# Weights split a unit ahead, low parts written over their landing slots, and a second mixer that begins with half of its value columns

## What is computed

```python
for i in range(DEPTH):                      # DEPTH = 2
    mix = ssd_mixer(x, ...) if i == 0 else hgrn2_mixer(x, ...)
    h = layer_norm(ALPHA * x + mix, ln_g[i, 0], ln_b[i, 0])
    h = layer_norm(ALPHA * h + square(relu(h @ mlp_w1[i])) @ mlp_w2[i], ln_g[i, 1], ln_b[i, 1])
    x = h + sigmoid(h @ ple_w_gate[i]) * (p[i] @ ple_w_proj[i])
```

## Time and profile before

| | |
|---|---|
| median of 3 runs | 2112.82 us (2112.81 to 2113.82) |
| the profiled execution's own time | 2113.44 us |
| its span in the profile | 2111.6 us |
| mean granted clock of PE | 0.967 |
| PE busy | 1975.9 us (94%) |
| DVE busy | 1072.6 us (51%) |
| ACT busy | 871.8 us (41%) |
| POOL busy | 173.3 us (8%) |

### The profile page before, as it was taken

One profiled execution on the slowest core, in us unless ns is written; L12 is line 12 of the kernel. 1 busy time (PEld: TensorE's weight loads), 2 busy tenths in 40 slices (PEclk: granted clock), 3 DMA queues, 4 the chain that ended last, 5 costly groups with the idle time before them and its releaser, 6 DMA issues.

```text
span 2111.6 us, 26519 instructions
## 1 busy us (share of the span) xinstructions
PE 1975.9 (94%) x9594; PEld 1572.8 (74%) x9594; DVE 1072.6 (51%) x1891; ACT 871.8 (41%) x1734; POOL 173.3 (8%) x137
## 2 busy tenths in 40 slices
PE   7999999979999999899898689999999879989998
PEld 6788887878888887688888577888887655447773
DVE  4666666355344344467677554343446342035643
ACT  5665664253333225366575534233334220114430
POOL 0110110030000003001010040000004000001100
PEclk9999999999999999999999799999999979988999
DMA  5131124313232220413121122222231212110010
GB/s 186 41 100 60 41 80 156 123 61 120 80 118 81 96 103 20 120 42 79 40 80 41 60 88 93 80 103 96 81 118 45 86 53 100 64 40 1 0 40 40
DMA packets 116542, 161.31 MB, mean 76 GB/s; under 512 B 6021, under 2 KB 57059, under 8 KB 116451
## 3 DMA queue, kind: packets, MB, share of 16 engines
q1 hardware_dynamic: 115155, 155.38, 22.1%
q0 software_dynamic: 1296, 4.72, 0.6%
HBM read 157.98 MB, written 2.10 MB: 76 GB/s over the span
## 4 chain that ended last, share of the span: by engine, by line
PE 82%; DVE 9%; ACT 5%; issue 2%; DVEq 1%; ACTq 1%; DMA 0%; SPq 0%; POOLq 0%; POOL 0%
PE psum L885 42%; PE psum L660 8%; PE psum L986 7%; PE psum L1141 4%; PE psum L625 4%; PE psum L848 3%; PE psum L1222 2%; PE psum L1176 2%; PE psum L1018 2%; PE psum L1189 2%; PE psum L965 1%; PE psum L809 1%; DVE z_lo L1782 1%; DVE w_lo L1992 1%; ACT fT L1279 1%
## 5 line engine op out<-in xcount | busy, mean ns | idle before, releaser
L1992 DVE TENSOR_TENSOR w_lo<-slot,w_hi 128x512 fp32r<-128x512 f32 x304 | 214.0, 719 | 377.4 <-ACT w_hi L1448 377.4
L1448 ACT CAST w_hi<-slot 128x512 fp32r<-128x512 f32 x304 | 183.7, 620 | 446.9 <-PE psum L885 446.2
L885 PE MATMUL psum<-f_hi,w_hi 128*128 128x512 f32 (+1 forms) x576 | 214.4, 372 | 21.4 <-issue 8.5
L885 PE MATMUL psum<-f_lo,w_hi 128*128 128x512 f32 (+1 forms) x576 | 213.5, 371 | 0.0
L885 PE MATMUL psum<-f_hi,w_lo 128*128 128x512 f32 (+1 forms) x576 | 213.2, 370 | 0.0
L885 PE MATMUL psum<-w_hi,hid_hi 128*128 128x512 f32 x512 | 199.5, 390 | 0.0
L885 PE MATMUL psum<-w_hi,hid_lo 128*128 128x512 f32 x512 | 199.2, 389 | 0.0
L885 PE MATMUL psum<-w_lo,hid_hi 128*128 128x512 f32 x512 | 199.2, 389 | 0.0
L885 PEld LDWEIGHTS psum<-f_hi,w_hi 128*128 128x128 f32 x576 | 111.7, 194 | 40.2 <-issue 8.9
L625 PE MATMUL psum<-con,arena 128*128 128x128 f32 (+2 forms) x710 | 106.1, 288 | 23.4 <-ACT arena L1695 8.2
L885 PEld LDWEIGHTS psum<-f_hi,w_lo 128*128 128x128 f32 x576 | 111.7, 194 | 17.6
(11 more groups left out here) (309 smaller groups left out, 4118.9 us busy)
## 6 DMA issues: line engine op xcount, KB each, us to landing
slot<-in_w_mlp SPq DMA_DIRECT2D x128, 512.0 KB, 5.5
slot<-in_w_ssd SPq DMA_DIRECT2D x32, 512.0 KB, 5.6
slot<-in_w_hgrn SPq DMA_DIRECT2D x32, 512.0 KB, 6.6
slot<-in_w_ssd_out SPq DMA_DIRECT2D x16, 512.0 KB, 6.2
slot<-in_w_gate SPq DMA_DIRECT2D x16, 512.0 KB, 5.2
gb<-in_w_ssd SPq DMA_DIRECT2D x8, 512.0 KB, 8.3
slot<-in_w_hgrn_out SPq DMA_DIRECT2D x8, 512.0 KB, 5.3
slot<-in_w_mla SPq DMA_DIRECT2D x8, 512.0 KB, 5.5
```

The costliest lines, as they stand in the source:

```text
L885: m = pe.matmul(psum[:, bank[c], cols or slice(0, HALF)], a, m_, start=opens and k == 0 and n_pass == 0, stop=closes and k == KD - 1 and n ...
L1448: act.copy(w_hi[:, k, :], as_k(slot_of(stage, n))[:, k, :]).then_inc(high_made, 1)
L1992: dve.tensor_tensor(w_lo[:, k, :], as_k(slot_of(stage, n))[:, k, :], w_hi[:, k, :].bitcast(F32), ALU.subtract).then_inc(low_made, 1)
```

## The change

High parts get two buffers (`w_his`; the second lies where `w_lo` was). The low parts lose theirs: `w_los` are views of the two landing slots, and DVE writes the low part over the landed values. A split now waits for PE's blocks of two units before; a slot is given back piece by piece, as PE begins the block behind a piece.

DVE no longer splits the next unit in one go ahead of tile 3, but in portions behind each of the four norms: 2, 2, 1, 3 blocks before an MLP, 3, 3, 2, 0 before a gate. ACT makes all eight high parts behind the square root of tile 0, and takes half of the turned values ahead of each root. In an MLP's first half product the turn of tile 3 moves to the middle (`halfway`). In `ssd_out` the last two tiles of the second half trade banks.

The second mixer's first weights are split in the order 2, 0, 1, on ACT ahead of the turned values, on DVE inside `ple` behind tile 1. PE projects part 2 once two tiles are ready, turns tile 3 behind it, and then makes parts 0, 1, 3 (before: 0, 1, 2, 3).

```diff
+MLP_SPLITS, GATE_SPLITS = (2, 2, 1, 3), (3, 3, 2, 0)
...
-        w_hi, w_lo = part("w_hi", 17920, KD, HALF), part("w_lo", 22016, KD, HALF)
+        w_his = [part(f"w_hi{n}", 17920 + n * KD * HALF, KD, HALF) for n in range(2)]
+        w_los = [x_lo, z_lo]
...
+                    if by_piece:
+
+                        sp.wait_ge(blocks_begun, split_units.index(u - 2) * KD + ((c + 1) * step + 1) + i * (per * KD))
+                        sp.sem_inc(sig("slot_given"), 1)
                     sp.dma_start(dst[:, c * step:(c + 1) * step, :], w(c * step, step)).then_inc(done, 16)
...
-                up(0, 0, slice(0, T // 2), ends=False)
-                last_turn()
+                up(0, 0, slice(0, T // 2), ends=False, halfway=last_turn)
...
-            for n in range(4):
-                hgrn_project(0, 0, n)
+            for t in range(NT - 1):
+                turn_rows("turn0", res, t, sig("ple_done0"), t + 1)
+            input_ready(2)
+            hgrn_project(0, 0, 2, 0)
+            turn_rows("turn0", res, NT - 1, sig("ple_done0"), NT)
+            input_ready(NT)
+            hgrn_project(0, 0, 0, 1)
+            hgrn_project(0, 0, 1, 2)
+            hgrn_project(0, 0, 3)
...
-                        act.wait_ge(blocks_begun, (u - 1) * KD + (k + 2) + i * (per * KD))
-                    act.copy(w_hi[:, k, :], as_k(slot_of(stage, n))[:, k, :]).then_inc(high_made, 1)
+                        act.wait_ge(blocks_begun, (u - 2) * KD + (k + 2) + i * (per * KD))
+                    act.copy(parts_of(stage, n)[0][:, k, :], as_k(slot_of(stage, n))[:, k, :]).then_inc(high_made, 1)
...
+                    if t > 0 and parts:
+                        turned_out(stage, t - 1, gain, bias)
...
+                    if t == 0 and split_next:
+                        split_next()
...
+            landed(act, "hgrn", 0)
+            for c in (2, 0, 1):
+                split_cols_high(0, c)
             for t in range(NT):
                 turned_out("turn0", t)
                 input_parts("turn0", t)
-                if t == 1:
-                    landed(act, "hgrn", 0)
-                    split_cols_high(0, 0)
-            split_cols_high(0, 1)
-            split_cols_high(0, 2)
...
-                        if before_last:
-                            before_last()
                     add(t)
                     dve.drain()
                     norm(t, rn[:, t, :], rn[:, t, :], LN_EPS, True).then_inc(norm_ready, 1)
                     if 1 < t < NT - 1:
                         input_parts(t - 2)
-                    if t == 1 and meanwhile:
-                        meanwhile()
+                    split_low(split_next, ks=range(sum(counts[:t]), sum(counts[:t + 1])))
...
+                    if t == 1 and meanwhile:
+                        meanwhile()
...
+            ple(0, first_cols_low)
```

More of the change, by code:

```diff
@@ L482, in load @@
             def load(view, w, stage, n=0, i=0, per=0):
-                s, done = slot_free(stage, n, i, per)
+                u = unit0[stage] + n
+                by_piece = stage in in_parts and u - 2 in split_units
+                s, done = (slots[u % 2], units_landed[u % 2]) if by_piece else slot_free(stage, n, i, per)
                 nk = view[1]
@@ L879, in times_parts @@
                         ready(k)
+                    if halfway and k == KD // 2:
+                        halfway()
                     for c in cs:
@@ L947, in gate_results @@
                 def gate_results(h, **results):
+                    w_hi, w_lo = parts_of(f"gate{i}", h)
                     times_parts(f"gate{i}", h, lambda t, k: (f_hi[:, k, t * P:(t + 1) * P], f_lo[:, k, t * P:(t + 1) * P],
@@ L971, in _, with hgrn_project @@
             ple(0, mlp(0, last_turn))
[L972 to L977, removed]
+            input_ready = next_input()
+            def hgrn_project(par, i, n, nth=None):
                 h = 2 * i + par
+                w_hi, w_lo = w_his
                 if n < 3:
-                    pe.wait_ge(sig("cols_low"), h * 3 + (n + 1))
+                    pe.wait_ge(sig("cols_low"), h * 3 + ((n if nth is None else nth) + 1))
                 def passes(out, hi_lo, k):
@@ L1455, in input_parts, with norm @@
                 act.copy(f_hi[:, :, tokens], fT[:, :, tokens]).then_inc(input_high, 1)
-            def norm(stage=None, gain=None, bias=None, parts=False, meanwhile=None, before_last=None):
+            def norm(stage=None, gain=None, bias=None, parts=False, split_next=None):
                 n = norms[0]
@@ L1512, in mlp @@
                 quarter(QUARTERS - 1, last=True)
-                norm(f"norm{i}1", B_G + 16 * i + 8, B_B + 16 * i + 8, parts=True, before_last=lambda: split_high(f"gate{i}"))
+                norm(f"norm{i}1", B_G + 16 * i + 8, B_B + 16 * i + 8, parts=True, split_next=lambda: split_high(f"gate{i}"))
             def ple(i):
@@ L1520, in ple @@
                         act.activation(sg[:, t, h * HALF:(h + 1) * HALF], psum[:, b, :], ACT.Sigmoid).then_inc(bank_free[b], 1)
-            norm("norm00", B_G, B_B, parts=True, before_last=lambda: split_high("mlp0"))
+            norm("norm00", B_G, B_B, parts=True, split_next=lambda: split_high("mlp0"))
             for i in range(DEPTH):
@@ L1646, in _ @@
                 act.copy(o_hi[:, k, :], oT[:, k, :]).then_inc(sig("o_high"), 1)
-            split_high("hgrn_out", 1)
-            norm("norm10", B_G + 16, B_B + 16, parts=True, before_last=lambda: split_high("mlp1"))
+            split_high("hgrn_out", 1, follows=False)
+            norm("norm10", B_G + 16, B_B + 16, parts=True, split_next=lambda: split_high("mlp1"))
             mlp(1)
@@ L1985, in _, with split_low @@
             inputs_split = [0]
-            def split_low(stage, n=0, i=0, per=0):
+            def split_low(stage, n=0, i=0, per=0, ks=range(KD)):
                 first = (part0[stage] + n) * KD
-                for k in range(KD):
+                w_hi, w_lo = parts_of(stage, n)
+                for k in ks:
                     dve.wait_ge(high_made, first + (k + 1) + i * (per * KD))
@@ L2101, in last_out_low, with split_cols_low, first_cols_low @@
                     out_low(3, k)
[L2103 to L2104 removed]
+            mixer_and_norm("ssd_out", "mlp0", last_out_low)
             mlp(0)
[L2106 to L2109 removed]
+            def split_cols_low(par, h, c, nth=None):
+                dve.wait_ge(sig("cols_high"), h * 3 + ((c if nth is None else nth) + 1))
                 cols = slice(c * P, (c + 1 + (c == 2)) * P)
+                w_hi, w_lo = w_his
                 dve.tensor_tensor(w_lo[:, :, cols], as_k(slot_of("hgrn", par))[:, :, cols], w_hi[:, :, cols].bitcast(F32),
                                   ALU.subtract).then_inc(sig("cols_low"), 1)
+            def first_cols_low():
+                for nth, c in enumerate((2, 0, 1)):
+                    split_cols_low(0, 0, c, nth)
+            ple(0, first_cols_low)
             for t in range(NT):
@@ L2254, in _ @@
             split_low("hgrn_out", 1)
-            mixer_and_norm("hgrn_out", name=lambda h, t: ((h, t), 0),
-                           before_last=lambda: split_low("mlp1"))
+            mixer_and_norm("hgrn_out", "mlp1")
             mlp(1)
```

55 lines of the change are left out of this document (22 added, 33 removed).

## The result

The changed kernel takes 2141.93 us (median; 2140.74 to 2142.62) where the kernel before takes 2112.82: a ratio of 1.0137, 95% interval 1.0119 to 1.0154. It is slower, as forecast, but by 29 us and not by 9, and it lies 5 us above the upper end of the range. Its profiled execution has a span of 2140.8 us, 29.2 more than that of before.

What follows compares the result with a forecast made beforehand. PE, busy 94%, was taken to bound the kernel, with changes only at four norm stretches and the second mixer's start. 4.4 + 8.4 - 5.5 - 5.5 - 10.5 = -8.7 us: 2112.8 becomes 2121.5 us, range 2104 to 2137.

Steps and rivals of the forecast that it cites:

- the low part over the slot is the same instruction with another address: Low parts written over the landing slots: listed among what was costed at nothing.
- only three things can change the time: PE, busy 94% of 2111.6 us: only a wait removed, a wait added, or a stretch at another clock matters.
- Turns of DVE and POOL: Norm stretches: two-SBUF-operand DVE instructions and POOL's run one after the other; about twenty low parts of 2.5 to 2.9 us.
- Before the MLPs: Norm stretches ahead of `mlp0` and `mlp1`: PE starts earlier, gains of 4.4 and 8.4 us.
- Before the gates: Ahead of `gate0` and `gate1`: late additions make PE wait, loss 4.3 us each, up to 2.8 more; taken 5.5 twice.
- Second mixer: Its start: PE pauses behind v and g and before the first level; loss 9.7 to 12.5 us, taken 10.5.
- Rival 1: Norm stretches: low parts slip past POOL and additions are on time; 33 us faster, 2080 us; chance 0.12.
- Rival 4: MLPs: slots come back late and each of 32 units waits 1 us; 2150 us; chance 0.03.
- Rival 3: Gates go worse: cold clocks in every new pause, PE behind DVE for all the first head; 2131 to 2138 us; chance 0.10.

Runs made afterwards that it cites:

- m2_offsets: Matmuls alone, none of the reference, single operands shifted by 0 to 256 bytes: two units took 43.51 us unshifted, 44.37 us with the stationary low part 224 bytes off.
- e2_in_place_only: Kernel before with only low parts written over the landing slots, each slot given back by piece: 2127.37 us, ratio 1.0064.
- e5_same_remainder: Changed kernel with the eight small tensors allocated ahead of the slots, so all large buffers share the arena's remainder: 2125.49 us, ratio 1.0060.
- e3_pool_late: Changed kernel with one more wait: POOL begins a residual only when all four tiles of the norm stretch have their f_lo; 2098.94 us, ratio 0.9927.
- e4_mixer_back: Changed kernel with the second mixer's start as before on PE, ACT and DVE: 2126.50 us, ratio 1.0050.
- m1_places: Matmuls alone, none of the reference, operands at chosen byte offsets: two units took 44.38 us with the stationary low part at the changed kernel's first slot.

## Why the prediction was wrong

**The step that failed** is "the low part over the slot is the same instruction with another address", costed at nothing. Behind it stands the premise that "only three things can change the time": a wait removed, a wait added, or a stretch at another clock. A fourth was left out, the pace of matmuls that wait for nothing at full clock. I looked at what the steady part waits for, and for waits it was right that nothing changes there: PE is busy without a gap. But the address has a price of its own, on PE and not on DVE that writes there: 0.43 us per unit of 96 matmuls. It is 12.3 us in the two MLPs, some 0.9 of the 1.5 in `hgrn_out` and 0.7 in the rest of each gate (both by `e2_in_place_only`), so about 15 of the 20 us by which the forecast missed. Shown by `m2_offsets`, which has nothing but the offsets, by `e2_in_place_only`, which brings it alone, and by `e5_same_remainder`, which takes it away. I hadn't named it among the rivals either. In the trace of before it could be seen: matmuls of `ssd_out` were 0.2333 us apart on average over the three passes with `yT_hi_a`, which lies in `fT`, and 0.2272 with `yT_hi_b` in the arena.

**Turns of DVE and POOL**: right, to about half a microsecond. The two traces are 0.25 us apart there: the gate's tile 0 was to begin at 807.3 and began at 808.07, tile 3's rows were to end at 817.8 and ended at 818.06. Of the 304 low parts of the units, 22 took over 1.5 us (up to 2.90); I had said about twenty. When both wait, the two engines take turns, one instruction each: three low parts in 6.30 us with two of POOL's (2.70 and 2.73) among them, and eight in 19.49 us in `e3_pool_late`. The Trainium skill ("SBUF — State Buffer", section "SBUF: two separate sides") says that of an instruction of VectorE with two SBUF inputs and one of GpSimd that reads SBUF, the one that starts first holds the port pair that they share for its whole length. The trace and `e3_pool_late` agree; the turns are what the page leaves open.

**Before the MLPs**: -5.2 and -9.4 for -4.4 and -8.4, right.

**Before the gates**: +4.6 and, before `gate1`, +5.3 (31.94 for 26.62) against my lower bound of 4.3, right. The rest of each gate lost 2.3 and 2.6 more. In `e2_in_place_only` and `e3_pool_late`, which have the offsets but no new pause there, the rest of `gate0` takes 38.90 us, 0.7 more than before. So 0.7 of the 2.3 are the offsets, and the other 1.6 go with the low clock behind the pause (0.76 in the window above). My chosen 5.5 was too small for either gate (6.9 and 7.9), and the second lies above my upper bound of 7.1 too.

**Second mixer**: the mechanism was right (pauses of 3.01, 3.18 and 4.05 us; I had 3.1 for the second), the size too small. 11.7 us to the first level for 10.5, and 2.7 more behind it (`e4_mixer_back`) that I had put at nothing: PE comes out of its pause at a low clock (0.74 from 920 to 924 us, 0.89 from 924 to 930) and gives time away in the first products of the recurrence.

**Rival 1**, low parts that slip past POOL, didn't happen, but `e3_pool_late` made it happen. I had worked out 13.2, 17.1 and twice 6.7 us against before; it gained 14.2, 17.7, 6.5 and 6.6 by the stretches of the table. The same arithmetic priced both cases well; what decides between them is one wait.

**Rival 4**, a stall of 1 us per unit since slots come back late, named the right place, a loss in every MLP unit, with more than twice the size (0.43 us came) and the wrong mechanism. No wait appears in the steady part, and the pieces land 3.6 us behind their issue.

**Rival 3**, cold clocks in the new pauses, came in part: it is in the 1.6 us of the gate and in the second mixer's 2.7.

## What to carry to other kernels

"The same instruction with another address" has to be looked at once for every engine that reads the address. Divide a stage's time by its matmuls before and after a change: a busy share of 100% hides a slower pace. If matmuls that alternate between operands take turns at different offsets, try allocating all of them at the same remainder of 256 bytes; here that cost nothing and gave 16 us.

Before work is moved on VectorE into a stretch where GpSimd is busy in SBUF, ask whether GpSimd's work could wait. One wait, on work that nobody needs until much later, turned 29 us of loss into some 15 us of gain, and the collisions went on where PE didn't wait for them; the offsets and the second mixer's old start, whose order had covered PE, gave 35 us more (2098.9 to 2063.5).

## What the hardware showed that I had not expected

- Matmuls of 128x128 by 512 columns in three passes, with nothing else running (`m1_places`, `m2_offsets`): 0.2266 us apart with all operands at one remainder of 256 bytes, 0.2289 to 0.2333 with one or two of four at another. At remainders 32, 96 and 160 off, the stationary low part cost more (44.65 to 44.80 us) than at 64, 128, 192 and 224 (44.37 to 44.38). Distance (186 KB) and multiples of 256 cost nothing.
- The Trainium skill (same page and section) says that DMA and engine accesses to SBUF can't contend. The runs agree: the slow pace is the same 44.37 us with a DMA share of 0.29 (the changed kernel) and with none (`m2_offsets`, 224 bytes).
